# A hybrid decoder step on one core: two value tiles of the sample cache go to other buffers, and four places of attention's order change

## The chip, the cores and the metric

The kernel runs on one core of a Trainium2 chip. The time is device microseconds of one execution; the median of several executions is quoted. The names of the engines are those of the profile: PE is TensorE, DVE is VectorE, ACT is ScalarE, POOL is GpSimd, and SP is SyncE, which here only requests transfers.

## The reference, cut to what matters

One layer is computed for two groups that share the weights: 512 prompt tokens, and 8 samples with one token each. After the token mixers comes cross-attention with 4 heads of width 256 over 256 memory tokens. For the prompt, keys and values are computed from `mem_prompt`. For the 8 samples they are read from a cache in HBM, and this is what the change is about:

```python
h = rms_norm(x, lp["g_x_pre"])
q = (h @ lp["w_q"]).reshape(B, T, N_XHEADS, XHEAD_DIM)
s = jnp.einsum("bthd,bmhd->bhtm", q, mem_k) * (XHEAD_DIM ** -0.5)
pr = jax.nn.softmax(s, axis=-1)
o = jnp.einsum("bhtm,bmhd->bthd", pr, mem_v).reshape(B, T, D_MODEL)
x = x + rms_norm(o @ lp["w_o_x"], lp["g_x_post"])
```

The feed-forward layer (1024 to 2 x 2816 and back) follows.

## The kernel before, in words

Every product of a weight matrix is made from halves of float32: ACT writes the high part of a weight block (`split_hi`, line 550), POOL or DVE the low part (`split_lo`, lines 837 and 2681), and PE runs three matmuls for each of 8 row tiles (hi x hi, hi x lo, lo x hi). A weight block is 128 columns. `piece` (line 496) computes one block for one half of the tokens, `dense` (line 514) for both halves. All orders are written out by hand: each engine has its own list of calls, and semaphores join them.

In attention, the prompt's part goes head by head: `scores(h)` on PE, `head_max(h)` on DVE (two reductions, then a small scaling), `exps(h)` on ACT (four exponentials), `head_norm(h)` on DVE (a reciprocal and four multiplications in `y_buf`), `turn_probs(h)` on PE (eight transposes), `take_prob_t(h)` on ACT, `weigh(h)` on PE, `o_high(h)` on ACT and `o_low(h)` on DVE. The turned probabilities of heads 0 to 2 lie in `prob_t`; the last head's not yet turned ones lie in rows 6 and 7 of `y_buf`. `weigh(h)` counts up the semaphore `weighed`, and `turn_probs(h)` counts up `prob_turned`.

The samples' part runs on DVE between these steps. `sample_scores(b)` multiplies two key tiles (t = 2b and 2b + 1, each 128 x 1024, 512 KB) by the query of sample b, which a transfer has spread over 128 partitions in `q_bc[:, b % 2]`. A tile costs four operations with an accumulator read each (line 2913). Then `sample_max`, `sample_exps`, `sample_norm` and `sample_columns` follow for each half g of the samples, and PE multiplies by the value tiles, t = 16 to 31, in `sample_values(g)`.

Key and value tiles share a ring of 11 slots in `cache`. SP requests them in order, all on one queue, and before each request it waits for the use of the tile that lay in the slot before (`k_used` for key tiles, `v_used` for value tiles). Between them it requests the spread queries: the one of sample b when `k_used` has reached 2(b - 1). So tiles 27 to 31 are requested when PE has used value tiles 16 to 20.

The output projection `w_o_x` is blocks `B_O` to `B_O + 7`. PE runs its first-half pieces (`o_piece(m, 0)`) between the steps of the samples' part. `o_piece(0, 1)` is the first that needs the samples' attention output; PE waits in front of it for `o_lo`, the low part of that output. Ahead of `turn_sample_scores(0)` PE waits for `o_low(3)`:

```python
            o_piece(1, 0, ks=range(0, KT - 2))
            pe.wait_ge(o_lo, XH)
            turn_sample_scores(0)
```

DVE's list puts `sample_scores(5)` ahead of that `o_low(3)`:

```python
            o_low(2)
            sample_scores(5)
            o_low(3)
            split_lo(B_O + 4)
            sample_max(0)
```

`branch_piece` on ACT (line 2065) squares and copies a finished piece, and so frees its PSUM bank.

Of the kernel before, what the change touches and what calls it, by code (L numbers as in the profile page):

```python
# [10 lines left out]
D = 1024  # L11
KT = D // P
# [10 lines left out]
TAPS = 31  # L23
MEM = 256
CACHE_SLOTS = 11
XH, XHD = 4, D // 4
FF = 2816
FT = FF // P
# [19 lines left out]
B_O = 86  # L48
# [7 lines left out]
TOK = ((slice(0, TOK_S), slice(TOK_S, NT)), (slice(TOK_S, NT), slice(0, TOK_S)), (slice(0, TOK_S), slice(TOK_S, NT)))  # L56
TOK_N = ((TOK_S, NT - TOK_S), (NT - TOK_S, TOK_S), (TOK_S, NT - TOK_S))
# [84 lines left out]
def hybrid_step_kernel(nc, A, O):  # L142
# [34 lines left out]
    h_hi = buf("h_hi", [P, KT, NT], F32R)  # L177
    h_lo = buf("h_lo", [P, KT, NT], F32R)
# [109 lines left out]
    y_buf = buf("y_buf", [P, KT, NT])  # L288
# [16 lines left out]
    prob_t = buf("prob_t", [P, 2, T])  # L305
    assert cursor[0] <= small_base
    cursor[0] = attn_base
    cache = buf("cache", [P, CACHE_SLOTS, D])
# [36 lines left out]
    ps = nc.alloc_psum_tensor("ps", [P, 8, 512], F32)  # L345

    def sem(name):
        return nc.alloc_semaphore(name)
# [5 lines left out]
    out_taken = [sem("out_taken0"), sem("out_taken1")]  # L354
# [91 lines left out]
    def freed(b):  # L446
# [18 lines left out]
            return b - 5  # L465
        return b - 1

    def probs(h):

        rows = y_buf[:, 2 * h:2 * h + 2].rearrange("p k n -> p (k n)")[:, 0:T // P * MEM]  # L470
        return rows.rearrange("p (t m) -> p t m", m=MEM)
# [73 lines left out]
    def split_hi(b, more=0, more4=0):  # L545
        nc.scalar.wait_ge(w_landed[b % RAW_SLOTS], 16 * (b // RAW_SLOTS + 1) + 16 * more4)
        if freed(b) is not None:
            nc.scalar.wait_ge(block_done, freed(b) + more)
        kts = block_kts(b)
        nc.scalar.activation(weights(b)[0][:, 0:kts], w_raw[:, b % RAW_SLOTS, 0:kts], ACT.Copy).then_inc(w_hi_ready, 1)  # L550
# [63 lines left out]
    post_squares, post_added, post_stats_mm = sem("post_squares"), sem("post_added"), sem("post_stats_mm")  # L614
    post_rsqrt, post_x_ready = sem("post_rsqrt"), sem("post_x_ready")
    branch_scaled = sem("branch_scaled")

    a_done, a_taken, up_taken = sem("a_done"), sem("a_taken"), sem("up_taken")
    attn_exp, attn_max, conv_hi, conv_lo = sem("attn_exp"), sem("attn_max"), sem("conv_hi"), sem("conv_lo")
# [34 lines left out]
    with nc.Block() as block:  # L654
        @block.sync
        def _(sp):
# [60 lines left out]
            def load_cache(t):  # L717
                name, j = ("cache_mem_k", t) if t < 2 * B else ("cache_mem_v", t - 2 * B)
                if t == 0:
                    sp.wait_ge(x2_turned, 9)  # L720
                    sp.wait_ge(mem_stored, 32)
                if t == 9:
                    sp.wait_ge(block_done, B_Q)
                if t == 5:
                    sp.wait_ge(block_done, finished(B_Q + 1))
                if t >= CACHE_SLOTS:
                    old = t - CACHE_SLOTS
                    if old < 2 * B:
                        sp.wait_ge(k_used, old + 1)
                    else:  # L730
                        sp.wait_ge(v_used, old - 2 * B + 1)
                src = A[name][0][j // 2].rearrange("(m p) h d -> m p (h d)", p=P)[j % 2]
                sp.dma_start(cache[:, t % CACHE_SLOTS], src).then_inc(cache_landed[t % CACHE_SLOTS], 16)

            for m in range(KT):
                load(B_Q + m, weight_view("w_q")[:, :, P * m:P * m + P])
# [7 lines left out]
            sp.wait_ge(q_stored, 16)  # L744
            t = CACHE_SLOTS
            for b in range(B):
                if b >= 2:
                    sp.wait_ge(k_used, 2 * (b - 1))
                sp.dma_start(q_bc[:, b % 2], q_scratch[b].partition_broadcast(P)).then_inc(q_landed[b % 2], 16)
                if b == 1:  # L750
                    for m in range(4, 6):
                        load(B_O + m, weight_view("w_o_x")[:, :, P * m:P * m + P])
                while t < 4 * B and t - CACHE_SLOTS < 2 * (b - 1):
                    load_cache(t)
                    t += 1
            while t < 4 * B:
                load_cache(t)
                t += 1
            for m in range(6, KT):
                load(B_O + m, weight_view("w_o_x")[:, :, P * m:P * m + P])  # L760
# [109 lines left out]
        def _(pe):  # L870
# [403 lines left out]
            b = B_GB + 6  # L1274
# [225 lines left out]
            def sample_values(g):  # L1500

                pe.wait_ge(prob_z_ready, g + 1)
                for b in range(B // 2 * g, B // 2 * (g + 1)):
                    for m in range(2):
                        t = 2 * B + 2 * b + m
                        pe.wait_ge(cache_landed[t % CACHE_SLOTS], 16 * (t // CACHE_SLOTS + 1))
                        for h in range(XH):
                            mm = small(ps[32 * h:32 * h + 1, 4 + b // 2, XHD * (b % 2):XHD * (b % 2 + 1)],
                                       prob_c[:, m, XH * b + h:XH * b + h + 1],
                                       cache[:, t % CACHE_SLOTS, XHD * h:XHD * (h + 1)], start=(m == 0), stop=(m == 1))  # L1510
                        mm.then_inc(v_used, 1)

            def turn_outputs(g):
# [33 lines left out]
            def o_piece(m, h, ks=every, x_ready=None):  # L1547
                b = B_O + m
                taken = (out_taken[b % 2], b // 2) if h else (a_taken, 11 + m) if m >= 2 else None
                piece(pe, b, h, h_hi, h_lo, ks, taken=taken)  # L1550

            for h in range(XH - 1):
                pe.wait_ge(o_lo, h + 1)
                o_piece(0, 0, ks=range(2 * h, 2 * h + 2))
# [14 lines left out]
            turn_outputs(0)  # L1569
            o_piece(5, 0, ks=range(3, KT))  # L1570
            turn_outputs(1)
            pe.wait_ge(o_lo, XH + 1)
            o_piece(0, 1)
            for j in range(N_SHIFT):
                mm = tr(ps[0:1 + B, 4 + j // 4, P * (j % 4):P * (j % 4) + P], p_last[:, j, :], ident[:, :])
            mm.then_inc(state_turned, 1)
# [109 lines left out]
        def _(act):  # L1686
# [378 lines left out]
            def branch_piece(t, b, m, h):  # L2065

                n = piece_no(t, m, h)
                act.wait_ge(*((a_done, 13 + m if t else m - 1) if h == 0 else (block_done, b + 1)))
                if n >= 2:
                    act.wait_ge(post_added, n - 1)  # L2070
                if h is None:
                    go(two(sq_tmp[:, n % 2]), out_view(b % 2), ACT.Square).then_inc(post_squares, 1)
                    go(two(y_buf[:, m]), out_view(b % 2), ACT.Copy).then_inc(out_taken[b % 2], 1)
                else:
                    go(sq_tmp[:, n % 2, TOK[t][h]], half_view(b, h), ACT.Square).then_inc(post_squares, 1)
                    go(y_buf[:, m, TOK[t][h]], half_view(b, h), ACT.Copy).then_inc(out_taken[b % 2] if h else a_taken, 1)
# [124 lines left out]
            def sample_exps(g):  # L2201
                act.wait_ge(attn_max, XH + g + 1)
                go(prob_s[:, :], ps[0:B * XH // 2, 6, 0:MEM], ACT.Exp, scale=XHD ** -0.5, bias=stat_s[:, g, 0:1],
                   accum_out=stat_s[:, g, 1:2]).then_inc(attn_exp, 1)
# [34 lines left out]
            act.wait_ge(mem_stored, 32)  # L2239
            split_hi(B_O + 4)  # L2240
            split_hi(B_O + 5)
            sample_exps(0)
            branch_piece(1, B_O, 0, 0)
            branch_piece(1, B_O + 1, 1, 0)
            branch_piece(1, B_O + 2, 2, 0)
            branch_piece(1, B_O + 3, 3, 0)
# [143 lines left out]
        def _(dve):  # L2390
# [285 lines left out]
            def split_lo(b):  # L2676

                dve.wait_ge(w_hi_ready, b + 1)
                dve.wait_ge(w_lo_ready, b)
                hi, lo = weights(b)  # L2680
                tt(lo, w_raw[:, b % RAW_SLOTS], hi.bitcast(F32), ALU.subtract).then_inc(w_lo_ready, 1)
# [201 lines left out]
            def head_max(h):  # L2883
                for t in range(0, T // P, 2):
                    dve.wait_ge(score_mm, 4 * h + t + 2)
                    ins = V.tensor_reduce(stat[:, 0, 4 * h + t:4 * h + t + 2],
                                          ps[:, 4 + 2 * (h % 2) + t // 2, :].rearrange("p (t m) -> p t m", m=MEM),
                                          AX.X, ALU.max, negate=True)
                link_v(ins)
                ts(stat[:, 0, 4 * h:4 * h + 4], stat[:, 0, 4 * h:4 * h + 4], XHD ** -0.5, None, ALU.mult  # L2890
                   ).then_inc(attn_max, 1)

            def head_norm(h):
                dve.wait_ge(attn_exp, 4 * h + 4)
                link_v(V.reciprocal(stat[:, 1, 4 * h:4 * h + 4], stat[:, 1, 4 * h:4 * h + 4]))
                for t in range(T // P):
                    ins = ts(probs(h)[:, t], probs(h)[:, t], stat[:, 1, 4 * h + t:4 * h + t + 1], None, ALU.mult)  # L2897
                ins.then_inc(prob_ready, 1)

            def o_low(h):  # L2900
                dve.wait_ge(o_hi, h + 1)
                tt(h_lo[:, 2 * h:2 * h + 2, B:NT], head_banks(h), h_hi[:, 2 * h:2 * h + 2, B:NT].bitcast(F32), ALU.subtract
                   ).then_inc(o_lo, 1)
# [35 lines left out]
            sample_scores(2)  # L2939
            head_norm(1)  # L2940
            head_max(2)
            split_lo(B_O + 3)
            o_low(0)
            head_norm(2)
            head_max(3)
            sample_scores(3, (0,))
            head_norm(3)
            o_low(1)
            sample_scores(3, (1,))
            sample_scores(4)  # L2950
            o_low(2)
# [125 lines left out]
```

## Time and profile before

| | us |
|---|---|
| median of 3 executions | 1090.45 |
| lowest and highest of them | 1088.4 and 1091.57 |
| the profiled execution, its own time | 1088.82 |
| its span | 1087.1 |
| PE busy | 1068.1 |
| DVE busy | 559.9 |
| ACT busy | 447.5 |
| POOL busy | 348.4 |

The span is the time between the first and the last instruction of the profiled execution; its own time has 1.7 us more around it. A row of a timeline gives the start in us from the span's start, the duration, the engine, the line, the operation, output and input, and in brackets how long the engine sat idle before it and who released it. Attention's part around the change lies from 586 to 654 us.

### The profile page before, as it was taken

What the parts mean: (1) busy time and instruction counts of PE and PEld (TensorE: products, weight loads), DVE (VectorE), ACT (ScalarE), POOL (GpSimd) and SP (SyncE); (2) the same over time, 40 slices, a digit from 0 to 9 for tenths busy, and PEclk for the clock granted to TensorE, in tenths of its full rate; (3) what the DMA queues carried; (4) which work ended last, traced back from release to release, by engine and by line L of the source; (5) the groups of instructions that cost most, each with busy time, mean ns of one, the idle gap of its engine ahead of it and who ended that gap; (6) DMA issues with size and microseconds to landing.
All of it is one profiled execution on the core that took longest, in us unless ns stands there. A gap on an engine that the chain in (4) does not pass through costs nothing.

```text
span 1087.1 us, 26532 instructions
## 1 busy us (share of the span) xinstructions
PE 1068.1 (98%) x11415; PEld 1007.2 (93%) x11415; DVE 559.9 (51%) x990; ACT 447.5 (41%) x780; POOL 348.4 (32%) x174
## 2 busy tenths in 40 slices
PE   8999999999999999999999999999999999999998
PEld 7998899998998997999999679899999999999998
DVE  5488788777785757874642943633232232200004
ACT  6454534434443677335553525723222222222232
POOL 3431331322311400645332003313344344344450
PEclk9999999999999999999999999999999999999999
DMA  7321121221213443565247783312323332332322
GB/s 221 90 77 34 58 61 42 60 78 41 68 41 114 124 137 96 196 199 150 59 156 236 245 315 94 97 54 79 92 83 94 96 89 84 92 88 87 92 68 80
DMA packets 163757, 115.96 MB, mean 107 GB/s; under 512 B 5304, under 2 KB 153034, under 8 KB 163401
## 3 DMA queue, kind: packets, MB, share of 16 engines
q1 hardware_dynamic: 159979, 104.87, 31.5%
q10 hardware_dynamic: 3686, 9.75, 2.5%
q8 instruction: 72, 1.18, 0.5%
q14 instruction: 20, 0.16, 0.0%
HBM read 108.91 MB, written 6.17 MB: 106 GB/s over the span
## 4 chain that ended last, share of the span: by engine, by line
PE 81%; DVE 8%; ACT 4%; issue 3%; DMA 2%; POOL 1%; DVEq 0%; ACTq 0%; POOLq 0%
PE ps L514 53%; PE ps L969 11%; PE ps L496 10%; PE ps L1614 3%; DVE conv_y L2477 2%; POOL w_lo L837 1%; DMA cache<-in_cache_mem_v_dram 1%; DVE cache L2913 1%; ACT w_hi L550 1%; DVE ps L2826 1%; DMA x_tok<-in_x_prompt_dram 1%; PE ps L558 0%; DVE m_lo L594 0%; DVE y_buf L2897 0%; PE ps L916 0%
## 5 line engine op out<-in xcount | busy, mean ns | idle before, releaser
L837 POOL TENSOR_TENSOR w_lo<-w_raw,w_hi 128x1024 fp32r<-128x1024 f32 (+2 forms) x122 | 287.7, 2359 | 562.8 <-ACT w_hi L550 562.8
L514 PE MATMUL ps<-h_hi,w_hi 128*128 128x260 f32 x1324 | 277.7, 291 | 1.3 <-POOL w_lo L837 1.0
L514 PE MATMUL ps<-h_hi,w_lo 128*128 128x260 f32 x1324 | 266.3, 283 | 0.0
L514 PE MATMUL ps<-h_lo,w_hi 128*128 128x260 f32 x1324 | 266.1, 282 | 0.0
L514 PEld LDWEIGHTS ps<-h_hi,w_hi 128*128 128x128 f32 x1324 | 204.2, 188 | 11.3 <-issue 5.5
L514 PEld LDWEIGHTS ps<-h_hi,w_lo 128*128 128x128 f32 x1324 | 204.0, 188 | 0.0
L514 PEld LDWEIGHTS ps<-h_lo,w_hi 128*128 128x128 f32 x1324 | 203.6, 188 | 0.0
L550 ACT ACTIVATE w_hi<-w_raw 128x1024 fp32r<-128x1024 f32 (+2 forms) x132 | 130.6, 991 | 165.0 <-PE ps L514 158.5
L2477 DVE SCALAR_TENSOR_TENSOR conv_y<-glu,prm,conv_y 128x512 f32<-128x512 f32 x120 | 103.9, 866 | 2.5
L2811 DVE TENSOR_TENSOR sq_acc<-sq_acc,sq_tmp 128x264 f32<-128x264 f32 (+2 forms) x35 | 28.0, 800 | 116.1 <-ACT sq_tmp L2343 76.0
L3018 DVE TENSOR_TENSOR f_tmp<-ps,silu 128x520 f32<-128x520 f32 x19 | 13.3, 699 | 137.7 <-PE ps L514 137.7
L969 PE MATMUL ps<-big 64*64 64x128 f32 (+1 forms) x1920 | 65.3, 240 | 1.2 <-DVE big L2498 1.0
L837 POOL TENSOR_TENSOR wx_lo<-w_raw,wx_hi 128x1024 fp32r<-128x1024 f32 x12 | 28.7, 2396 | 106.1 <-ACT wx_hi L550 106.1
L969 PEld LDWEIGHTS ps<-big 64*64 64x64 f32 x1920 | 51.1, 134 | 7.1 <-DVE big L2498 1.5
L514 PE MATMUL ps<-f_lo,w_hi 128*128 128x260 f32 x264 | 53.1, 283 | 0.0
L514 PE MATMUL ps<-f_hi,w_hi 128*128 128x260 f32 x264 | 53.1, 282 | 0.0
L514 PE MATMUL ps<-f_hi,w_lo 128*128 128x260 f32 x264 | 53.1, 283 | 0.0
L3022 DVE TENSOR_TENSOR f_lo<-f_tmp,f_hi 128x520 f32 (+1 forms) x19 | 43.0, 2261 | 17.7 <-ACT f_hi L2296 17.7
L2291 ACT ACTIVATE silu<-ps 128x520 f32<-128x520 f32 x19 | 11.5, 606 | 75.2 <-PE ps L514 75.2
L496 PE MATMUL ps<-h_hi,wx_hi 128*128 128x264 f32 (+1 forms) x140 | 40.9, 292 | 1.1 <-DVE h_lo L2974 0.7
L514 PEld LDWEIGHTS ps<-f_hi,w_lo 128*128 128x128 f32 x264 | 40.7, 188 | 0.0
L514 PEld LDWEIGHTS ps<-f_hi,w_hi 128*128 128x128 f32 x264 | 40.7, 188 | 0.0
(497 smaller groups left out, 2090.0 us busy)
## 6 DMA issues: line engine op xcount, KB each, us to landing
w_raw<-in_w_gate_up_dram SPq DMA_DIRECT2D x44, 512.0 KB, 3.7
w_raw<-in_w_in_dram SPq DMA_DIRECT2D x38, 512.0 KB, 3.7
cache<-in_cache_mem_k_dram SPq DMA_DIRECT2D x16, 512.0 KB, 6.4
cache<-in_cache_mem_v_dram SPq DMA_DIRECT2D x16, 512.0 KB, 6.4
w_raw<-in_w_down_dram SPq DMA_DIRECT2D x16, 512.0 KB, 4.1
w_raw<-in_w_k_dram SPq DMA_DIRECT2D x8, 512.0 KB, 4.1
w_raw<-in_w_v_dram SPq DMA_DIRECT2D x8, 512.0 KB, 3.7
w_raw<-in_w_out_dram SPq DMA_DIRECT2D x8, 512.0 KB, 4.1
```

The source lines that it names most:

```text
L496: mm = nc.tensor.matmul(ps[:, 2 * (b % 2) + h, 0:TOK_N[t][h]], w[:, k, :], x[:, k, TOK[t][h]], start=(k == 0 and n == 0), stop=(k == KT - ...
L514: mm = nc.tensor.matmul(ps[:, 2 * s + a, 0:width], w[:, k, :], x[:, x0 + k, a * width:(a + 1) * width], start=(first and k == 0 and n == 0 ...
L550: nc.scalar.activation(weights(b)[0][:, 0:kts], w_raw[:, b % RAW_SLOTS, 0:kts], ACT.Copy).then_inc(w_hi_ready, 1)
L837: pool.tensor_tensor(lo[:, 0:kts], w_raw[:, b % RAW_SLOTS, 0:kts], hi[:, 0:kts].bitcast(F32), ALU.subtract).then_inc(w_lo_ready, 1)
L969: return nc.tensor.matmul(out, lhsT, rhs, start=start, stop=stop)
L1614: mm = nc.tensor.matmul(ps[:, 2 * (m % 2) + h, 0:TOK_N[2][h]], w[:, k, :], x[:, k0 + k, TOK[2][h]], start=(j == 0 and k == 0 and n == 0), ...
L2291: go(two(silu[:, :]), out_view(0), ACT.Silu).then_inc(out_taken[0], 1)
L2477: link_v(stt(conv_y[:, p, 0:T], src, w, conv_y[:, p, 0:T], ALU.mult, ALU.add))
L2811: ins = tt(sq_acc[:, cols], sq_acc[:, cols], sq_tmp[:, n % 2, cols], ALU.add)
L2826: ins = stt(ps[:, 4 + k % 2, 0:width], y_buf[:, k, cols], prm_col(gain, k), ps[:, 6, 0:width], ALU.mult, ALU.mult)
L3018: tt(two(f_tmp[:, j % 2]), out_view(1), two(silu[:, :]), ALU.mult).then_inc(out_taken[1], 1)
L3022: tt(f_lo[:, at].rearrange("p o n -> p (o n)"), f_tmp[:, j % 2], f_hi[:, at].rearrange("p o n -> p (o n)").bitcast(F32), ALU.subtract).the ...
```

## The change: what it does

1. Value tiles 27 and 28 (sample 5, second tile; sample 6, first tile) no longer go to the ring. Tile 27 goes to `prob_t`, tile 28 to rows 6 and 7 of `y_buf`. SP requests both ahead of the spread query of sample 5, after `weighed` has reached 3 and `prob_turned` has reached 4. Their landings count on a semaphore of their own, and `sample_values(1)` reads them there. Tiles 29 to 31 wait as before.
2. `o_piece(0, 1)` becomes `first_o_piece`: the 16 matmuls with the high part of the activations come first, after a wait for `o_hi`; the 8 with the low part come last, after the wait for `o_lo`. The number of matmuls stays 24.
3. ACT runs `branch_piece(1, B_O, 0, 0)` ahead of `sample_exps(0)`.
4. DVE runs `head_max(3)` ahead of `head_norm(2)`, and `split_lo(B_O + 3)` behind `o_low(1)` where it stood ahead of `o_low(0)`.

```diff
@@ -23,6 +23,8 @@
 CACHE_SLOTS = 11
+
+APART = (27, 28)
@@ -465,6 +467,14 @@
+    def cache_tile(t):
+
+        if t == APART[0]:
+            return prob_t[:, :, :].rearrange("p m t -> p (m t)")
+        if t == APART[1]:
+            return y_buf[:, 6:8].rearrange("p k n -> p (k n)")[:, 0:D]
+        return cache[:, t % CACHE_SLOTS]
@@ -723,14 +734,18 @@
-                if t >= CACHE_SLOTS:
+                if t == APART[0]:
+                    sp.wait_ge(weighed, XH - 1)
+                elif t == APART[1]:
+                    sp.wait_ge(prob_turned, XH)
+                elif t >= CACHE_SLOTS:
                     old = t - CACHE_SLOTS
...
-                sp.dma_start(cache[:, t % CACHE_SLOTS], src).then_inc(cache_landed[t % CACHE_SLOTS], 16)
+                sp.dma_start(cache_tile(t), src).then_inc(apart_landed if t in APART else cache_landed[t % CACHE_SLOTS], 16)
@@ -744,6 +759,9 @@
             t = CACHE_SLOTS
             for b in range(B):
+                if b == 5:
+                    for apart in APART:
+                        load_cache(apart)
                 if b >= 2:
                     sp.wait_ge(k_used, 2 * (b - 1))
@@ -754,7 +772,8 @@
             while t < 4 * B:
-                load_cache(t)
+                if t not in APART:
+                    load_cache(t)
                 t += 1
@@ -1503,11 +1522,14 @@
-                        pe.wait_ge(cache_landed[t % CACHE_SLOTS], 16 * (t // CACHE_SLOTS + 1))
+                        if t in APART:
+                            pe.wait_ge(apart_landed, 32)
+                        else:
+                            pe.wait_ge(cache_landed[t % CACHE_SLOTS], 16 * (t // CACHE_SLOTS + 1))
@@ -1549,6 +1571,19 @@
+            def first_o_piece():
+
+                hi, lo = weights(B_O)
+                out = ps[:, 2 * (B_O % 2) + 1, 0:TOK_N[1][1]]
+                pe.wait_ge(out_taken[B_O % 2], B_O // 2)
+                for k in range(KT):
+                    for n, w in enumerate((hi, lo)):
+                        nc.tensor.matmul(out, w[:, k, :], h_hi[:, k, TOK[1][1]], start=(k == 0 and n == 0), stop=False)
+                pe.wait_ge(o_lo, XH + 1)
+                for k in range(KT):
+                    mm = nc.tensor.matmul(out, hi[:, k, :], h_lo[:, k, TOK[1][1]], start=False, stop=(k == KT - 1))
+                mm.then_inc(block_done, 1)
@@ -1569,8 +1604,8 @@
             turn_outputs(1)
-            pe.wait_ge(o_lo, XH + 1)
-            o_piece(0, 1)
+            pe.wait_ge(o_hi, XH + 1)
+            first_o_piece()
@@ -2239,8 +2274,8 @@
+            branch_piece(1, B_O, 0, 0)
             sample_exps(0)
-            branch_piece(1, B_O, 0, 0)
@@ -2939,13 +2974,13 @@
             head_max(2)
-            split_lo(B_O + 3)
             o_low(0)
+            head_max(3)
             head_norm(2)
-            head_max(3)
             sample_scores(3, (0,))
             head_norm(3)
             o_low(1)
+            split_lo(B_O + 3)
             sample_scores(3, (1,))
```

On SP, whose rows are its requests, the place around the spread query of sample 5. Before, with the query in row 97:

```order
96 L733 DMA cache<-in_cache_mem_v_dram 128x1024 [waits k_used]
97 L749 DMA q_bc<-q_scratch 128x1024 [waits k_used]
98 L733 DMA cache<-in_cache_mem_v_dram 128x1024 [waits k_used] x2
99 L749 DMA q_bc<-q_scratch 128x1024 [waits k_used]
102 L733 DMA cache<-in_cache_mem_v_dram 128x1024 [waits k_used] x6
103 L733 DMA cache<-in_cache_mem_v_dram 128x1024 [waits v_used] x5
```

In the changed kernel:

```order
96 L748 DMA cache<-in_cache_mem_v_dram 128x1024 [waits k_used]
97 L748 DMA prob_t<-in_cache_mem_v_dram 128x1024 [waits weighed]
98 L748 DMA y_buf<-in_cache_mem_v_dram 128x1024 [waits prob_turned]
99 L767 DMA q_bc<-q_scratch 128x1024 [waits k_used]
100 L748 DMA cache<-in_cache_mem_v_dram 128x1024 [waits k_used] x2
104 L748 DMA cache<-in_cache_mem_v_dram 128x1024 [waits k_used] x6
105 L748 DMA cache<-in_cache_mem_v_dram 128x1024 [waits v_used] x3
```

The two requests apart now stand, with their two waits, ahead of the query; of the five that wait for `v_used`, three are left.

On DVE, the place behind `head_max(2)`, whose scaling is row 559; `stat` holds maxima and sums, `h_lo<-ps,h_hi` is `o_low`, and `w_lo<-w_raw,w_hi` is `split_lo(B_O + 3)`. Before:

```order
559 L2890 TENSOR_SCALAR stat<-stat 128x4 [waits dve_chain]
560 L2681 TENSOR_TENSOR w_lo<-w_raw,w_hi 128x1024 [waits w_lo_ready,w_hi_ready]
561 L2902 TENSOR_TENSOR h_lo<-ps,h_hi 128x2x512 [waits o_hi]
562 L2895 RECIPROCAL stat<-stat 128x4 [waits attn_exp]
563 L2897 TENSOR_SCALAR y_buf<-y_buf,stat 128x256 [waits dve_chain]
565 L2886 TENSOR_REDUCE stat<-ps 128x2 [waits score_mm] x2
566 L2890 TENSOR_SCALAR stat<-stat 128x4 [waits dve_chain]
567 L2913 ISA cache,sc<-cache,q_bc 128x256 [waits cache_landed6,q_landed1]
```

In the changed kernel, this place and the one behind `head_norm(3)`:

```order
559 L2925 TENSOR_SCALAR stat<-stat 128x4 [waits dve_chain]
560 L2937 TENSOR_TENSOR h_lo<-ps,h_hi 128x2x512 [waits o_hi]
561 L2921 TENSOR_REDUCE stat<-ps 128x2 [waits score_mm] x2
562 L2925 TENSOR_SCALAR stat<-stat 128x4 [waits dve_chain]
563 L2930 RECIPROCAL stat<-stat 128x4 [waits attn_exp]
566 L2948 ISA cache,sc<-cache,q_bc 128x256 [waits cache_landed6,q_landed1]
...
577 L2937 TENSOR_TENSOR h_lo<-ps,h_hi 128x2x512 [waits o_hi]
578 L2716 TENSOR_TENSOR w_lo<-w_raw,w_hi 128x1024 [waits w_lo_ready,w_hi_ready]
579 L2948 ISA cache,sc<-cache,q_bc 128x256 [waits cache_landed7,q_landed1]
```

The last head's maxima moved ahead of head 2's normalisation, and the weight's low part moved behind two normalisations, the first key tile of sample 3 and `o_low(1)`.

## Rows read from the trace of the kernel before

**Rows 1.** The page's head and its busy times of PE.

```profile
span 1087.1 us, 26532 instructions
PE 1068.1 (98%) x11415; PEld 1007.2 (93%) x11415; DVE 559.9 (51%) x990; ACT 447.5 (41%) x780; POOL 348.4 (32%) x174
```

**Rows 2.** The page's chain that ended last, by engine.

```profile
PE 81%; DVE 8%; ACT 4%; issue 3%; DMA 2%; POOL 1%; DVEq 0%; ACTq 0%; POOLq 0%
```

**Rows 3.** PE's timeline, 607 to 628 us.

```profile
613.88 1.04 PE L1470 MATMUL ps<-ident,y_buf 128*128 128x128 f32 x8
615.75 1.09 PE L1470 MATMUL ps<-ident,y_buf 128*128 128x128 f32 x8 [0.83 <-DVE y_buf L2897]
616.68 3.60 PE L969 MATMUL ps<-prob_t,v_tok 128*128 128x512 f32 x8
...
627.79 0.38 PE L1491 MATMUL ps<-ident,sc 128*16 128x128 f32 x2
```

**Rows 4.** PE's timeline, 598 to 610 us: the last heads' scores.

```profile
607.00 3.62 PE L969 MATMUL ps<-kt,y_buf 128*128 128x256 f32 x16
```

**Rows 5.** PE's timeline, 630 to 654 us: the idle times that end there.

```profile
630.06 0.36 PE L496 MATMUL ps<-h_hi,w_hi 128*128 128x256 f32 x1 [0.46 <-ACT y_buf L2076]
...
648.36 0.61 PE L969 MATMUL ps<-cache,prob_c 128*1 128x256 f32 x8 [0.64 <-DMA cache<-in_cache_mem_v_dram]
...
653.34 0.39 PE L496 MATMUL ps<-h_hi,wx_hi 128*128 128x264 f32 x1 [0.70 <-DVE h_lo L2974]
```

**Rows 6.** ACT's timeline, 628 to 653 us.

```profile
628.83 0.47 ACT L2203 ACTIVATE prob_s<-ps,stat_s 16x256 f32<-16x256 f32 x1 [2.16 <-DVE stat_s L2922]
...
629.56 0.36 ACT L2076 ACTIVATE y_buf<-ps 128x256 f32<-128x256 f32 x1
...
652.68 0.28 ACT L2255 ACTIVATE h_hi<-ps 128x32 fp32r<-128x32 f32 x2 [0.21 <-PE ps L1519]
```

**Rows 7.** DVE's timeline, 607 to 615 us.

```profile
607.32 1.23 DVE L2681 TENSOR_TENSOR w_lo<-w_raw,w_hi 128x1024 fp32r<-128x1024 f32 x1
608.46 1.22 DVE L2902 TENSOR_TENSOR h_lo<-ps,h_hi 128x1024 fp32r<-128x1024 f32 x1
...
609.80 1.14 DVE L2897 TENSOR_SCALAR y_buf<-y_buf,stat 128x256 f32<-128x256 f32 x4
610.86 1.28 DVE L2886 TENSOR_REDUCE stat<-ps 128x2 f32<-128x512 f32 x2
...
614.34 0.18 DVE L2895 RECIPROCAL stat<-stat 128x4 f32<-128x4 f32 x1 [0.58 <-ACT y_buf L2188]
```

**Rows 8.** DVE's timeline, 622 to 627 us: sample 5's scores and what follows.

```profile
622.55 0.43 DVE L2913 CUSTOM_DVE_ANT_0 cache<-cache,q_bc 128x256 f32<-128x256 f32 x1
...
625.32 1.22 DVE L2902 TENSOR_TENSOR h_lo<-ps,h_hi 128x1024 fp32r<-128x1024 f32 x1
```

**Rows 9.** SP's queue, 618 to 620 us, and its waits from 600 to 662 us.

```profile
618.23 0.33 SPq L749 DMA_DIRECT2D q_bc<-q_scratch  x1
...
SPq L749 <- DVE sc L2913: 22.3, 5, 12.2
```

**Rows 10.** Issue to landing (last number), requests of 618.23, 618.60 and 619.06 us.

```profile
q_bc<-q_scratch SPq DMA_DIRECT2D x1, 512.0 KB, 4.3
...
DMA to landing us min/median/max: 5.3/5.3/5.3
...
DMA to landing us min/median/max: 6.1/6.1/6.1
```

**Rows 11.** Windows of 0.5 us, PEclk behind POOL's; then PE's timeline, 9 to 20 us.

```profile
9.00:9.50 0.50, 0.45 (x3) 0.45 (x4) 0.50 (x2) 0.45 (x1) 0.00 (x0) 0.66 0.99 395
...
12.50:13.00 0.50, 0.50 (x6) 0.50 (x6) 0.50 (x2) 0.50 (x3) 0.50 (x1) 0.92 0.07 17
...
9.05 3.61 PE L906 MATMUL ps<-ident,x_tok 128*128 128x128 f32 x16 [2.13 <-DVE x_tok L2409]
...
18.52 1.09 PE L906 MATMUL ps<-ident,x_tok 128*128 128x128 f32 x8 [0.73 <-DVE x_tok L2409]
```

More of the change, by code:

```diff
@@ L616, in hybrid_step_kernel @@
     branch_scaled = sem("branch_scaled")
+    apart_landed = sem("apart_landed")
     a_done, a_taken, up_taken = sem("a_done"), sem("a_taken"), sem("up_taken")
@@ L1509, in sample_values @@
                                        prob_c[:, m, XH * b + h:XH * b + h + 1],
-                                       cache[:, t % CACHE_SLOTS, XHD * h:XHD * (h + 1)], start=(m == 0), stop=(m == 1))
+                                       cache_tile(t)[:, XHD * h:XHD * (h + 1)], start=(m == 0), stop=(m == 1))
                         mm.then_inc(v_used, 1)
```

## The prediction

> **What bounds the kernel now.** I read the page first. PE is busy for 1068.1 of 1087.1 us [rows 1], and 81% of the chain that ended last is PE's own work [rows 2]. The change removes no matmul: `first_o_piece` has the same 24, and `sample_values(1)` the same 64. So it can only give back idle time of PE inside attention, or add some. The second view is therefore PE's timeline there, for the gaps in front of its instructions. Four of them touch the places of the change: 0.83 us ahead of the last head's transposes, released by DVE's normalisation [rows 3]; 0.46 us ahead of `o_piece(2, 0)`, released by ACT's copy; 0.64 us inside `sample_values(1)`, released by the landing of a value tile; and 0.70 us ahead of `o_piece(0, 1)`, released by DVE's `h_lo` [rows 5]. Together they are 2.6 us, 0.24% of the time. That is the ceiling of any gain that the rows show. A measurement of this kernel can tell about 0.3% from no change, here 3.3 us, so even the whole ceiling would count as no change. The third view is the timeline of DVE, ACT and SP's queue around the same places, because a request that is moved can delay what stands behind it.
>
> **DVE's order (edit 4).** Before, DVE runs, from 607.32 us: the weight's low part, `o_low(0)`, head 2's normalisation, and only at 610.86 head 3's maxima [rows 7]. The scores of head 3 are there earlier: PE starts them at 607.00 and takes 3.62 us, so half of them is done near 608.8 and all of them at 610.62 [rows 4]. In the new order `o_low(0)` takes the place at 607.32 and is over near 608.5 (1.14 us, from the starts of its neighbours). The first reduction runs at once, the second (half of 1.28 us) from 610.65 to 611.3, and the small scaling ends near 611.5, where it was 610.86 + 1.28 + 0.2 = 612.35 before. So ACT's exponentials of head 3 end near 613.45, no longer just before 614.34 [rows 7]. But DVE has its other work still to do: normalisation of head 2 (0.2 + 1.14 us) to 612.8, four pieces of sample scores (8 take 2.77 us from 622.55 to 625.32 [rows 8], so 4 take 1.4) to 614.2, then the normalisation of head 3 to 615.45. It ended at 615.7 before. **The gain is 0.28 us** on the 0.83 us gap, not 0.83. The transposes of head 2 at 613.88 [rows 3] are covered, since their input is ready at 612.8.
>
> The bill comes behind it. DVE now idles some 1.5 us while it waits for scores, and the weight's low part is still to be made. `o_low(1)` ends near 616.6, the low part near 617.7, the second key tile of sample 3 near 619.1 (618.1 before), sample 4 near 621.9, and `o_low(2)` near 623.05. DVE is then ready for sample 5 at 623.05, 0.5 us later than the 622.55 of before [rows 8]. By itself that costs nothing: PE waits for `o_low(3)` in front of `turn_sample_scores(0)`, which would be ready at 623.05 + 2.77 + 1.22 = 627.05, and PE comes there at 627.79 - 0.28 = 627.51 [rows 3].
>
> **The two requests (edit 1).** The change is meant to use a pause of SP's queue. The pause is there: SP waited up to 12.2 us for the spread query of sample 5, which it issued at 618.23 [rows 9]. But the first of the two new requests waits until `weigh(2)` is done. Its matmuls start at 616.68 and take 3.60 us [rows 3]; 0.28 us earlier, they end at **620.0**. SP works in order, so the query of sample 5 now stands behind that wait, and behind two requests of 512 KB. Requests follow each other 0.37 to 0.46 us apart (issues at 618.23, 618.60 and 619.06), so the query is issued near 620.9, 2.7 us later than before and 1.8 us later than its own condition (619.1) would allow.
>
> It also lands later than its issue alone would say. The three requests from 618.23 went into an empty queue and landed 4.3, 5.3 and 6.1 us after their issues [rows 10], that is 4.3, 5.7 and 6.9 us after the first. The query is now the third of such a group that starts at 620.0, so **it lands near 626.9**; before, it was the first of its group and landed at 622.5. DVE was ready for it at 623.05. It waits 3.85 us, then makes sample 5's scores (2.77 us, to 629.7) and `o_low(3)` (1.22 us, to 630.9) [rows 8]. PE may go on at about 630.95 instead of 627.79: **+3.16 us**, a gap of some 3.4 us. Queued behind the waiting DVE are `split_lo(B_O + 4)`, `sample_max(0)` and all later steps, which PE needs 3 us or more after this place as it did before, so they move along with PE and add nothing further.
>
> The unknown is the landing. The lower bound: the query lands 4.3 us after its own issue as it did alone [rows 10], at 625.2; then the price is +1.5. The upper bound: one more transfer's step of 1.3 us (the steps of rows 10 are 1.2 to 1.4 us), at 628.2; then it is +4.5. I take 3.16, since the group of three in rows 10 is the same case.
>
> **What the tiles give.** Tiles 29 to 31 are still requested as PE uses tiles, but two transfers of 1.2 to 1.3 us each no longer stand ahead of them, and tiles 27 and 28 have landed long before. The 0.64 us wait [rows 5] goes: **-0.64**. Nothing is late next: after the delay above, the last request goes out near 641 and has until 650 to land.
>
> **ACT's order (edit 3).** `sample_exps(0)` held ACT from 628.83 for 0.47 us, and the copy that PE waited for ran from 629.56 [rows 6]. Moved ahead, the piece starts when its matmuls end, about six matmuls of 0.12 us and their tail behind 627.79 [rows 3], near 628.9. PE's gap of 0.46 shrinks to about 0.1: **-0.4**, with 0.3 and 0.46 as bounds. The exponentials start 0.4 us later; their consumer, the transposes of the probabilities, comes a whole piece of 3 us later.
>
> **`first_o_piece` (edit 2).** The two copies of `h_hi` end at 652.68 + 0.28 = 652.96 [rows 6], and PE started at 653.34 after DVE's part [rows 5]. It can start near 653.0, and the low part is there 16 matmuls before it is wanted: **-0.3** of the 0.70. It can't be the whole, since `h_hi` itself is awaited.
>
> **The sum**: 3.16 (which has the 0.28 in it) - 0.64 - 0.4 - 0.3 = **+1.8 us**. Against the profiled execution's own time of 1088.82 that is 1090.6; that execution lies 1.6 us below the median of the three, so against the median of 1090.45 it is **1092.2 us**. The own range of this case, from the landing's bounds, is 1090.6 to 1093.6.
>
> **Rivals.**
>
> A. *The clock falls in the new gap.* This ends slower. The trace shows it once: PE sat idle for 2.13 us up to 9.05 us, after sparse transposes, and its granted clock was 0.66 in the half microsecond from 9.0 and back at 0.92 in the one from 12.5 [rows 11], so 1.2 GHz for some 3.4 us. 16 transposes took 3.61 us there, where 8 took 1.09 at 2.4 GHz [rows 11], so 16 take 2.18: it cost 1.4 us in that stretch and, at half the rate, up to 1.7 us in 3.4. The new gap of 3.4 us is longer than that one. Against it: PE is busy up to the gap here, and it was not there. If it happens the time is 1092.2 + 1.7 = **1093.9**; it decides as soon as PE's gap ahead of `turn_sample_scores(0)` passes what the clock bears, some point above 0.83 us [rows 3], behind which PEclk stayed 1.00. The Trainium skill ("TensorE: Matmul & The Clock Gate", section "Why this matters for your kernels") speaks against this change by the same mechanism: it warns that a long idle gap between bursts of matmuls drops TensorE to half its clock. By that rule the result is 1093.9, by the row of the 0.83 us gap 1092.2. Chance 20%.
>
> B. *The query does not queue behind the tiles* and lands 4.3 us after its issue. Then the price is +1.5, the sum 1.5 - 0.64 - 0.4 - 0.3 = +0.2, the time **1090.6**. Rows 10 speak against it (the third took 6.1 us, not 4.3). The Trainium skill ("DMA: Bandwidth & Descriptors", "Queues, rings and completion order") says that a later transfer may complete before an earlier one of the same queue; by that rule alone this would be possible. Chance 12%.
>
> C. *The delay is hidden* and only the gains are left: -0.28 - 0.64 - 0.4 - 0.3 = -1.6, **1088.8**. For this the query would have to land by 623.5, that is, SP would have to pass the two waits before 617.6, or PE's wait for `o_low(3)` would have to have more slack than the 0.5 us that I find. Chance 16%.
>
> My forecast has the remaining 52%.
>
> **How the numbers follow.** Faster by over 0.3% means under 1087.2; only C with a lucky scatter of the runs (1088.4 to 1091.57 before) or a gain that I don't see reaches it: 6%. Slower by over 0.3% means over 1093.7: more than half of A, and the upper end of my own case: 20%. The rest, 74%, is no change. The range goes from just under C, 1088.3, to just over A, 1094.4.
>
> **What the profile after would show.** Right: SP's requests for `prob_t` and `y_buf` at about 620.0 and 620.5, the next `q_bc` near 620.9 with a landing of about 6 us; DVE idle 3 to 4 us ahead of sample 5's scores, released by that transfer; PE idle about 3.4 us ahead of the transposes of `sc`, released by DVE's `h_lo`; no wait for a value tile; gaps of about 0.55, 0.1 and 0.35 us in place of 0.83, 0.46 and 0.70. Wrong: a `q_bc` request before 619 us, or a DVE that reaches sample 5 without a wait (then C), PEclk under 1.00 behind 631 us (then A), or new gaps in the norms behind 660 us, for which I have no term.

## The result, and the profile after

| | before | changed |
|---|---|---|
| median of 20 executions | 1090.37 us | 1091.74 us |
| range | 1087.5 to 1092.5 | 1090.05 to 1095.64 |
| ratio, with its 95% interval | | 1.0018 [1.0011, 1.0025] |
| the profiled execution, its own time | 1088.82 us | 1091.12 us |

The changed kernel is 0.18% slower, about 2.0 us by the ratio and 1.4 us by the medians. By the bound of the prediction (0.3%) that is no change, but the interval leaves out 1. The forecast was 1092.2 us. Two executions far above all others, one of before at 1278.6 us (beside e5 to e8) and one of e6 at 2614.33 us, enter none of the ratios and ranges below.

The page of the changed kernel has a span of 1089.4 us (1087.1 before) and a busy PE for 1069.8 us of it (1068.1 before, [rows 1]), with the same 11415 matmuls. The same matmuls kept PE busy for 1.7 us longer, so part of the loss is a slower PE and not an idle one.

SP's queue from 619 to 621 us, then the issue to landing of the request for `q_bc` (last number; against [rows 9, 10]):

```profile
619.76 0.33 SPq L748 DMA_DIRECT2D prob_t<-in_cache_mem_v_dram  x1
620.13 0.43 SPq L748 DMA_DIRECT2D y_buf<-in_cache_mem_v_dram  x1
620.61 0.43 SPq L767 DMA_DIRECT2D q_bc<-q_scratch  x1
...
q_bc<-q_scratch SPq DMA_DIRECT2D x1, 512.0 KB, 5.7
```

DVE's timeline: sample 5's first score (against [rows 8]):

```profile
626.35 0.42 DVE L2948 CUSTOM_DVE_ANT_0 cache<-cache,q_bc 128x256 f32<-128x256 f32 x1 [3.66 <-DMA q_bc<-q_scratch]
```

PE's timeline, the same places as [rows 3 to 5]:

```profile
606.69 3.62 PE L988 MATMUL ps<-kt,y_buf 128*128 128x256 f32 x16
...
615.20 1.09 PE L1489 MATMUL ps<-ident,y_buf 128*128 128x128 f32 x8 [0.58 <-DVE y_buf L2932]
616.13 3.60 PE L988 MATMUL ps<-prob_t,v_tok 128*128 128x512 f32 x8
...
630.39 0.39 PE L1510 MATMUL ps<-ident,sc 128*16 128x128 f32 x2 [2.96 <-DVE h_lo L2937]
...
636.50 0.29 PE L1516 MATMUL ps<-ident,prob_s 16*128 16x16 f32 x2
...
655.62 0.39 PE L1581 MATMUL ps<-h_hi,wx_hi 128*128 128x264 f32 x1 [0.38 <-ACT h_hi L2290]
```

Windows behind the gap (busy times of PE, its weight loads, DVE, ACT and POOL, then PEclk, the granted clock as a share of 2.4 GHz):

```profile
627.50:630.30 2.80, 0.00 (x0) 0.00 (x0) 2.80 (x12) 0.00 (x0) 0.00 (x0) 1.00 1.02 415
630.30:631.00 0.70, 0.60 (x6) 0.59 (x7) 0.70 (x2) 0.00 (x0) 0.00 (x0) 1.00 1.05 427
631.00:634.30 3.30, 3.30 (x18) 3.30 (x17) 3.23 (x16) 1.74 (x6) 0.00 (x0) 0.50 1.02 416
634.50:640.00 5.50, 5.50 (x52) 5.09 (x54) 4.12 (x24) 0.79 (x3) 0.00 (x0) 1.00 0.84 311
```

A reader sees four things. The query of sample 5 is the third of a group, behind the two new requests, and lands at 620.61 + 5.7 = 626.3. DVE waits 3.66 us for it. PE waits 2.96 us for `o_low(3)`; no wait for a value tile is left. And 0.6 us after PE has started again its clock drops to 1.2 GHz for 3.4 us.

The two profiled executions can be compared place by place, since every step of PE is there in both. From before to changed: up to 607 us, -0.31 us, which the change has not touched. The gap ahead of head 3's transposes, from 0.83 to 0.58, -0.25. From `weigh(2)` (616.68, now 616.13) to the transposes of `sc` (627.79, now 630.39), the step grew from 11.11 to 14.26 us: +3.15. From there to the transposes of `prob_s` (633.06 in the timeline of before, now 636.50) it grew from 5.27 to 6.11. That +0.84 has two parts, and two other runs tell them apart. e5, with ACT's new order and no gap, takes 4.93 us for this step, and e2, with ACT's new order and the clock at 1.00, takes 4.94. So ACT's order gave 0.33 us and the low clock cost 1.17. The stretch with `sample_values(1)`, up to the transposes of its outputs, lost 0.83, and the wait ahead of `first_o_piece` 0.33 (0.70, now 0.38). The sum is -0.31 - 0.25 + 3.15 + 1.17 - 0.33 - 0.83 - 0.33 = +2.3 us, as the two own times say (1091.12 - 1088.82).

### The profile page after: what moved, and what is told of

It reads as the page before. It is cut to its first block, busy times and chain, and to the rows that moved or that the text cites. A ratio compares the mean times of both kernels' runs of the same rounds, so it can differ in the third digit from the quotient of the medians.

```text
span 1089.4 us, 26532 instructions
## 1 busy us (share of the span) xinstructions
PE 1069.8 (98%) x11415; PEld 1009.5 (93%) x11415; DVE 559.4 (51%) x990; ACT 447.5 (41%) x780; POOL 348.2 (32%) x174
## 4 chain that ended last, share of the span: by engine, by line
PE 82%; DVE 8%; ACT 4%; issue 3%; DMA 2%; POOL 1%; DVEq 0%; SPq 0%; ACTq 0%; POOLq 0%
PE ps L524 53%; PE ps L988 11%; PE ps L506 10%; PE ps L1649 3%; DVE conv_y L2512 2%; POOL w_lo L856 1%; DVE cache L2948 1%; DMA q_bc<-q_scratch 1%; ACT w_hi L560 1%; DVE ps L2861 1%; DMA x_tok<-in_x_prompt_dram 0%; PE ps L568 0%; DVE m_lo L604 0%; PE ps L935 0%; DVE y_buf L2932 0%
## 5 line engine op out<-in xcount | busy, mean ns | idle before, releaser
L524 PEld LDWEIGHTS ps<-f_lo,w_hi 128*128 128x128 f32 x264 | 40.6, 188 | 0.0
```

The costliest lines, as they stand in the source:

```text
L524: mm = nc.tensor.matmul(ps[:, 2 * s + a, 0:width], w[:, k, :], x[:, x0 + k, a * width:(a + 1) * width], start=(first and k == 0 and n == 0 ...
```

## The experiments

The theory after the result: the query of sample 5 stands behind a wait and two transfers, which opens a gap on PE, and the gap lets the clock fall; the other edits and the tiles' places pay. The rivals: the load of the two transfers costs wherever they stand; DVE's new order makes the gap; the clock adds nothing that can be measured. Each kernel was timed beside executions of before on the same chip.

**e1, the query first.** An edit of the changed kernel:

```diff
             for b in range(B):
-                if b == 5:
-                    for apart in APART:
-                        load_cache(apart)
                 if b >= 2:
                     sp.wait_ge(k_used, 2 * (b - 1))
                 sp.dma_start(q_bc[:, b % 2], ...
+                if b == 5:
+                    for apart in APART:
+                        load_cache(apart)
```

> The changed kernel, with one edit: the two requests for tiles 27 and 28 stand directly behind the spread query of sample 5, no longer ahead of it. Theory (the query's place in SP's list costs the time): the query is issued near 619, when its own condition holds, and lands near 623.4; DVE waits under 0.6 us for it, PE's gap ahead of the transposes of sc is under 0.4 us, PEclk stays 1.00 there, and the time is 1.0 to 1.6 us below before. Rival (the two transfers cost by the load they put on the DMA engines near 620 us, wherever they stand): PE's gap stays over 1.5 us, and the time stays above before.

Measured: 1087.34 us, ratio 0.9988 [0.9977, 0.9999]. The loss turned into a gain of 1.3 us by the ratio, 2.2 by the medians. The query went out at 618.93, DVE waited 0.59 us for it, and no gap is left ahead of the transposes of `sc`. PE's longest wait, 590 to 662 us, and DVE's waits for the queries of samples 5 and 6 show what is left:

```profile
PE ps L1516 <- DVE prob_s L2962: 0.8, 1, 0.8
...
623.40 0.43 DVE L2948 CUSTOM_DVE_ANT_0 cache<-cache,q_bc 128x256 f32<-128x256 f32 x1 [0.59 <-DMA q_bc<-q_scratch]
631.24 0.43 DVE L2948 CUSTOM_DVE_ANT_0 cache<-cache,q_bc 128x256 f32<-128x256 f32 x1 [2.22 <-DMA q_bc<-q_scratch]
```

The second wait is for the query of sample 6. It now stands behind the two tiles, beside the two of the ring that were ahead of it before, and took 9.3 us to land (5.7 before), so 0.8 us of a gap has moved to the transposes of `prob_s`. So the load of the transfers is not harmless; but what it costs PE here, 0.8 us, comes through the query that stands behind them, and is far less than the 2.96 us that their old place cost.

**e2 and e10, PE kept busy in the gap.** The changed kernel with 24 transposes ahead of the wait; it computes nothing that is used:

```diff
             o_piece(1, 0, ks=range(0, KT - 2))
+            keep_awake(24)
             pe.wait_ge(o_lo, XH)
             turn_sample_scores(0)
```

> The changed kernel, with 24 transposes of the identity into an unused PSUM bank put on PE ahead of its wait for o_low(3); their results are used by nobody. Theory (the gap lets TensorE's clock fall to 1.2 GHz in some executions, which costs up to 1.7 us on top of the gap): the transposes fill most of the gap, PEclk is 1.00 from 627 to 640 us in the profile, PE passes the place at the same time as in the changed kernel, and the median is 0.5 to 1.7 us below the changed kernel's, so 0.3 to 1.5 us above before. Rival (the clock adds nothing that can be measured, the gap alone is the price): the median is that of the changed kernel, 1.8 to 2.1 us above before, or higher.

> The changed kernel itself, beside e10 and on the same chip, to have the two side by side. Both theories: 1.4 to 2.5 us above before. The clock theory: most of its executions have a mean granted clock of 0.997 or less.

> e2 again, beside e9. Clock theory: the median is 0.5 to 1.7 us below e9's, and nearly all executions have a mean granted clock of 0.998 or more. Rival (e2's smaller loss was the chip's scatter): within 0.4 us of e9.

Measured: e2 1090.17 us, ratio 1.0008 [0.9999, 1.0016]. Side by side, e9 (the changed kernel) 1091.21 us, 1.0014 [1.0003, 1.0025], and e10 1090.35 us, 1.0005 [0.9996, 1.0015]. PE passes the place as late as before (630.52 us), but the clock holds. Two windows of e2, where the changed kernel has 0.00 busy and then PEclk 0.50:

```profile
627.50:630.30 2.80, 2.54 (x24) 2.30 (x22) 2.80 (x13) 0.00 (x0) 0.00 (x0) 1.00 1.01 413
631.00:634.30 3.30, 3.17 (x27) 3.00 (x26) 3.23 (x16) 1.62 (x6) 0.00 (x0) 1.00 1.02 385
```

The profiled executions give the price. In those of e9 and e2 PE starts the transposes of `sc` at the same 630.52 us. e9 comes to those of `prob_s` at 636.50, e2 at 635.46, and the spans end 1.0 us apart (1089.4 and 1088.4). The changed kernel takes 6.11 us for this step, e2 4.94: so the low clock costs 1.04 to 1.17 us, beside the gap.

How often the clock fell there in the other executions can only be estimated, since they have a mean granted clock in three digits and no trace. One stretch of 3.4 us at half the clock anywhere makes a mean of 0.998. The profiled execution of before has it (at its start only), and so has that of e3 (behind the gap only); the changed kernel's has both and 0.996. Averaged over executions the mean clock was 0.9972 in the 32 of the changed kernel and e9, 0.9988 in 95 of before and 0.9991 in the 23 of e2 and e10; 0.997 or less stands in 18, 12 and none of them. The difference between the first two, 0.0016 of 1089 us, is 1.7 us of full clock, as much as one such stretch takes away. So by this estimate the fall comes in most executions, more than the 18 that read 0.997 or less; the mean doesn't say at which place. The medians of e9 and e10 differ by 0.9 us; their intervals overlap, so the times alone don't settle the size. In e2's profiled execution the useless transposes delay nothing: PE still waits 0.49 us behind them.

**e3, the tiles alone.** The changed kernel with edits 2, 3 and 4 undone.

> The kernel before with edit 1 alone (the tiles apart, requested ahead of the query). Theory: the query lands near 627, DVE is ready for it at 622.55, PE's gap is 3.0 to 3.6 us, the wait for a value tile is gone; the time is 2.3 to 4.3 us above before, with the upper end where the clock falls. Rival (DVE's order is the cause of the gap): the gap is under 1 us and the time within 0.7 us of before.

Measured: 1092.96 us over 6 executions, ratio 1.0034 [1.0021, 1.0047], so 3.7 us above before, as expected. PE's gap is longer than expected. The query landed 6.7 us after its issue, 0.8 us later than in the changed kernel, and PE came 0.25 us earlier. The clock fell here too, as the window shows:

```profile
631.15 0.59 PE L1510 MATMUL ps<-ident,sc 128*16 128x128 f32 x2 [3.97 <-DVE h_lo L2937]
...
631.00:634.30 3.30, 3.15 (x15) 3.07 (x16) 3.23 (x14) 1.09 (x4) 0.00 (x0) 0.53 0.87 299
```

DVE's order is not the cause of the gap: without it the gap is there, and larger. The 3.7 us of edit 1 alone and the 1.6 us that the other three give in e4 below make +2.1, close to the 2.0 of the whole change.

**e4, everything but the tiles.** `APART` is empty, edits 2, 3 and 4 stay.

> The changed kernel without edit 1: all value tiles in the ring, edits 2, 3 and 4 kept. Theory: PE's gaps shrink from 0.83 to 0.55, from 0.46 to 0.1 and from 0.70 to 0.38 us, the 0.64 us wait for a value tile stays or grows by up to 1 us since PE comes earlier; the time is 0 to 1.0 us below before. Rival (DVE's order is the cause of the loss): the time is 1 us or more above before.

Measured: 1087.91 us, ratio 0.9985 [0.9973, 0.9998]: 1.6 us below before, more than the 1.0 expected at most. Its executions scatter from 1087.14 to 1091.42. The profiled one took 1090.49 us, in the upper part of that scatter, and shows one place where time was lost in it. PE in `sample_values(1)` and behind it, then a window:

```profile
646.05 0.61 PE L980 MATMUL ps<-cache,prob_c 128*1 128x256 f32 x8 [0.36 <-DMA cache<-in_cache_mem_v_dram]
647.32 0.61 PE L980 MATMUL ps<-cache,prob_c 128*1 128x256 f32 x8 [0.65 <-DMA cache<-in_cache_mem_v_dram]
648.83 1.03 PE L980 MATMUL ps<-cache,prob_c 128*1 128x256 f32 x8 [0.89 <-DMA cache<-in_cache_mem_v_dram]
649.79 1.97 PE L1533 MATMUL ps<-ident,o_rows 128*128 128x128 f32 x8
...
649.00:651.00 2.00, 2.00 (x14) 1.21 (x7) 0.00 (x0) 1.02 (x1) 0.00 (x0) 0.50 0.34 103
```

Three waits for value tiles, 1.9 us in all, where the profiled execution of before had 0.64, and behind them the clock at 1.2 GHz. DVE waited 0.43 us for the query of sample 5, issued at 618.54, and no gap stands ahead of the transposes of `sc`.

**e5 and e6, the orders in two parts.** The kernel before with edits 2 and 3 alone, and with edit 4 alone.

> The kernel before with edits 2 and 3 alone (first_o_piece, and the branch piece ahead of sample_exps(0)). Theory: the 0.46 us gap shrinks to about 0.1 and the 0.70 us gap to 0.38 us; PE comes 0.4 us earlier to sample_values(1), so the wait for value tiles grows from 0.64 us by up to 0.4 us. The time is 0.3 to 0.7 us below before, less than can be told. Rival (the gain of e4 came from these two): 1 us or more below before.

> The kernel before with edit 4 alone (DVE's order). Theory: head 3's transposes wait 0.55 us in place of 0.83, the query of sample 5 is requested near 619 in place of 618.2 and DVE waits under 0.6 us for it; the wait for value tiles stays at 0.5 to 1.0 us; the time is 0 to 0.4 us below before, so no difference. Rival (DVE's order pays on its own, and made the gain of e4): 1 us or more below before.

Measured: e5 1089.50 us, ratio 0.9992 [0.9978, 1.0006]; e6 1090.20 us, 0.9997 [0.9984, 1.001]. Both are no difference, and both intervals hold the small gains that were expected. In e6, DVE waited 0.46 us for the query, requested at 619.17, as expected. What was not expected stands on PE ahead of `o_piece(2, 0)`:

```profile
630.40 0.36 PE L496 MATMUL ps<-h_hi,w_hi 128*128 128x256 f32 x1 [1.00 <-ACT y_buf L2076]
```

It was 0.46 us before. DVE's new order makes `sample_exps(0)` later (629.17 us, 628.83 before, though PE is 0.19 us ahead), and ACT's old order has the copy behind it, so edit 4 alone adds 0.54 us at `o_piece(2, 0)`, against 0.25 us gained at head 3. With edit 3 beside it, in e4, this wait is gone.

e5's profiled execution waited 2.0 us for value tiles. The value tiles tell why these gains don't reach the end. In the five profiled executions with all tiles in the ring (before, e4, e5, e6, e11) the last wait for a tile ended between 648.4 and 649.5 us, while PE began `sample_values(1)` at 644.5 and 644.9 in before and e6 and at 643.4 to 643.9 in the other three. Where PE came earlier, it waited longer: 0.64 and 0.66 us against 1.5 to 2.0. By the ratios the two parts gain 0.9 and 0.3 us, so 1.2 of e4's 1.6; by the medians it is 0.4 better and 0.3 worse. The intervals are wider than these differences.

**e7, the pause really used.** The changed kernel; tile 28 ahead of the query of sample 5, tile 27 behind that of sample 6:

```diff
                 if b == 5:
-                    for apart in APART:
-                        load_cache(apart)
+                    load_cache(APART[1])
...
                 sp.dma_start(q_bc[:, b % 2], ...
+                if b == 6:
+                    load_cache(APART[0])
```

> The changed kernel with the two requests at other places: tile 28 (which needs only prob_turned, near 616.3) ahead of sample 5's query, so really in the pause of the queue, and tile 27 behind the query of sample 6. Theory (what costs is a query behind a wait and behind transfers): the query of sample 5 goes out near 619 and the one of sample 6 near 621.5, PE's gap ahead of the transposes of sc is under 0.4 us and the 0.8 us wait that e1 showed ahead of the transposes of prob_s goes, no wait for value tiles; the time is 0.3 to 0.8 us below e1 and 1.5 to 2.6 us below before. Rival (any request of 512 KB in this stretch delays a query by a transfer's 1.3 us): at or above e1.

Measured: 1087.13 us, ratio 0.9974 [0.9962, 0.9987], so 2.8 us below before, a little more than expected. It is 0.1% better than e1 by the ratios, whose intervals overlap, and 0.2 us by the medians, which are of two chips. Tile 28 went out at 615.75, the query at 618.25, the one of sample 6 at 621.02, and no wait for value tiles is left. One point was not as expected. In the profiled execution the query landed 5.9 us after its issue, DVE waited 2.06 us and PE 1.4 us ahead of the transposes of `sc`. Tile 28 had taken 4.3 us and was over at 620.05, so the query's own transfer overlapped it for 1.8 us. In e8 and e12, which have the same list on SP, the overlap was 1.1 us and the query took 4.4 and 4.5 us. So one execution has a query delayed by 1.6 us beside a tile, about what the rival says, and two have not.

**e8 and e12, head 3 first.** e7, and on DVE:

```diff
-            sample_scores(3, (0,))
             head_norm(3)
             o_low(1)
-            split_lo(B_O + 3)
-            sample_scores(3, (1,))
+            sample_scores(3)
             sample_scores(4)
             o_low(2)
             sample_scores(5)
             o_low(3)
-            split_lo(B_O + 4)
+            split_lo(B_O + 3)
...
             sample_columns(0)
+            split_lo(B_O + 4)
             sample_scores(7, (0,))
```

> As e7, and DVE normalises head 3 ahead of both key tiles of sample 3, with split_lo(B_O + 3) behind o_low(3) and split_lo(B_O + 4) behind sample_columns(0). Theory: the exponentials of head 3 end near 613.4, so its normalisation ends near 614.7 and the 0.55 us gap ahead of head 3's transposes goes; the other gaps stay as in e7 or grow by up to 0.3 us, since PE comes earlier. The time is 0.2 to 0.6 us below e7. Rival (DVE is now what bounds this stretch): the 0.55 us comes back as a longer wait for o_low(3), and the time is that of e7.

> e8 again, to see whether its gain holds beside a second set of executions of before: the ratio to before is between 0.9950 and 0.9975 if e8's gain is real, and above 0.9985 if it was scatter.

Measured: e8 1086.56 us, ratio 0.9963 [0.9947, 0.9978]; e12 1087.16 us, 0.9975 [0.9965, 0.9985]. The gain holds: 2.7 to 4.0 us below before, and it beats both kernels. Whether it beats e7 (0.9974) the intervals don't say. PE's waits of e8, 590 to 662 us, are down to one:

```profile
PE ps L1582 <- ACT h_hi L2291: 0.4, 1, 0.4
```

The normalisation of head 3 starts at 612.65 us, 0.75 us after DVE is free, as the exponentials end, and heads 2 and 3 are turned without a gap (16 transposes in one piece from 612.98 us). e12's profiled execution has, beside this wait, one of 0.3 us ahead of the transposes of `sc`.

In none of the 45 executions of e1, e7, e8 and e12 was the mean clock below 0.998 (in 12 of 95 of before it was), and all but one of them lie between 1085.8 and 1088.8 us, where those of before reach from 1086.9 to 1094.96.

**e11, the wait without the transfers.** e4, and on SP:

```diff
             for b in range(B):
+                if b == 5:
+                    sp.wait_ge(weighed, XH - 1)
```

> e4 (edits 2, 3 and 4, all tiles in the ring) with one wait added: SP waits for weighed to reach 3 ahead of the query of sample 5, as in the changed kernel, but no request goes between. It splits the query's delay in its two parts. Theory (half of the delay is the wait, half the two transfers ahead): the query is issued near 620.0, lands 4.3 us later near 624.4, DVE waits 1.2 to 2.0 us for it, PE's gap ahead of the transposes of sc is 0.6 to 1.4 us, against 3.0 in the changed kernel. The time is 0.5 to 1.5 us above e4's (1087.9 beside a before of 1089.55). Rival (the wait alone makes it): the gap is 2.5 us or more.

Measured: 1090.42 us, ratio 1.0006 [0.9995, 1.0016]. The query landed 4.1 us after its issue at 619.13, DVE waited 1.21 us and PE 0.5 us ahead of the transposes of `sc`:

```profile
623.28 0.43 DVE L2939 CUSTOM_DVE_ANT_0 cache<-cache,q_bc 128x256 f32<-128x256 f32 x1 [1.21 <-DMA q_bc<-q_scratch]
```

DVE's 3.66 us of the changed kernel have three parts. In e4, without wait and requests, it already waits 0.43. The wait for `weigh(2)` adds 0.78 of them, and the two requests ahead the other 2.45: 0.85 in issuing (619.76 to 620.61) and 1.6 in landing later (5.7 against 4.1 us). PE's steps say the same. From head 3's transposes to those of `sc` it takes 12.05 us in e4 (12.04 before), 12.76 in e11 and 15.19 in the changed kernel, so the wait costs PE 0.7 us and the requests 2.4. The theory said halves; it is one quarter and three quarters, and the gap was a little under the 0.6 us expected. The time is above the 0.5 to 1.5 us expected over e4 (2.3 by the ratios). The profile has 1.5 us of waits for value tiles, and 4 of 12 executions a clock of 0.997 or less. How much of the 2.3 us these made is open.

## Why the prediction was right, point by point

**The gap.** Right in place, cause and size. Foreseen were a request at 620.0, the query at 620.9 and its landing 6.0 us later; it was 619.76, 620.61 and 5.7 us, in an execution that was 0.31 us earlier. DVE was to wait 3.85 us and waited 3.66. The transposes of `sc` were to come 3.16 us later and came 630.39 - 627.79 + 0.31 = 2.91 us later. The wait for the landing of the third in a group [rows 10] was the right row: e11 shows that the query alone takes 4.1 us, and rival B, which said that it would not queue, is ruled out by the 5.7.

**The gains.** `first_o_piece` 0.33 (0.3 foreseen), head 3's gap 0.25 (0.28), ACT's 0.33 (0.4; within its bounds of 0.3 and 0.46). The tiles gave 0.83 us of that stretch, where the gap of 0.64 was foreseen. Without them the gains of the other edits are partly lost, since PE then comes earlier to tiles that land no earlier: e4, e5 and e11 waited 1.9, 2.0 and 1.5 us there. That edit 4 costs nothing by itself, as the prediction has it, holds only beside edit 3 (e6).

**The clock.** Here the step failed that gave rival A 20%. It was argued that PE is busy up to the gap, and it was not there for the 2.13 us gap at the start [rows 11]. The clock fell nevertheless, in both profiled executions of the changed kernel and in e3's, and by the estimate above in most others. PEclk under 1.00 behind 631 us was the prediction's own sign for rival A, so A's mechanism came and not the main case. The price was 1.04 to 1.17 us, below the 1.7 foreseen, and the time stayed far under A's 1093.9.

The main case had no term for the clock, and its number held all the same. The steps of the profiled executions give 2.91 - 0.33 - 0.83 - 0.33 = +1.4 us without the clock, where +1.8 was foreseen, and +2.6 with it. Of this the profiled pair shows +2.3, since 0.31 us had been gained ahead of the change, and the many executions +2.0 by the ratio and +1.4 by the medians. A missing term of +1.2 and a sum that was 0.4 too high partly cancelled, and the interval of the ratio (1.2 to 2.7 us) holds the +2.6. So the mechanism of the gap was foreseen, but that the time came within 0.5 us of 1092.2 is partly luck. The Trainium skill's warning ("TensorE: Matmul & The Clock Gate", section "Why this matters for your kernels") about idle gaps between bursts was the better guide: the trace agrees, PEclk 0.50 behind a gap of 2.96 us, and the gap filled with transposes keeps 1.00.

**Rival C**, the hidden delay with a gain of 1.6 us, did not occur. e1, where the query goes first, comes near its sum: 1.3 us by the ratio and 2.2 by the medians, with a new wait of 0.8 us.

## What to carry to other kernels

A pause of a queue can only take a request whose condition holds, and whose transfer ends, within it. A request whose wait ends behind the pause holds up everything that stands behind it in the same list, and then its transfer holds it up once more (here the transfers cost three times what the wait did); ask of each moved request what comes next in the list and who waits for that. A gap that opens on TensorE costs more than its length when it lets the clock fall. A wait for a transfer that lands at a fixed time grows by what is gained ahead of it, so it should be sized with the other edits in place.

## What the runs showed of the hardware

The granted clock fell to 0.50 not only behind one long gap. In e4 it fell behind three short ones (0.36, 0.65 and 0.89 us), with eight matmuls of one column of weights between each two, and eight transposes then took 1.97 us where they take 1.04 to 1.09 at 2.4 GHz. In e5 it fell behind one gap of 2.03 us at the same place, `sample_values(1)`. In the other direction, the gaps of 0.5 us in e11 and 1.4 us in e7 ahead of the transposes of `sc`, and e11's two waits for value tiles (0.41 and 1.08 us), did not make it fall in the profiled executions.

A query of 512 KB, first of its group, landed 4.1 to 4.5 us after its issue in eight profiled executions, as third of a group 5.7 to 6.7 us in five, and behind four other tiles 9.3 us (e1). Of the three with a tile still under way when the query was issued, e8 and e12 are among the eight; e7, with the longest overlap, had 5.9 us. Whether the overlap is the reason is open.
